# A hybrid attention and RWKV-7 trunk: the next head pair's front moved one round ahead, small products alternating between tiles of the PE array

## The chip, the cores and the metric

The kernel runs on one core of a Trainium2 chip. The metric is the device time of one execution in microseconds. Its engines are named as in the profile: PE (TensorE matmul), DVE (VectorE), ACT (ScalarE), POOL (GpSimd), SP (the DMA queue). Each runs its own list of instructions in program order; semaphores join them.

## The reference

Two layers over x (512 tokens, 1024 channels). A layer normalizes x, projects it once, and feeds two groups whose outputs are joined and projected back: softmax attention (4 heads) and a bidirectional RWKV-7 time mixing (8 heads of 64). A gated MLP with a width-3 convolution follows. The part that the change touches is the RWKV group:

```python
def wkv7_scan(r, w, k, v, kk, a, reverse):
    def step(state, inp):
        r_t, w_t, k_t, v_t, kk_t, a_t = inp
        sa = jnp.einsum('bhvk,bhk->bhv', state, -kk_t)
        state = (state * w_t[:, :, None, :] + sa[..., None] * (kk_t * a_t)[:, :, None, :]
                 + v_t[..., None] * k_t[:, :, None, :])
        return state, jnp.einsum('bhvk,bhk->bhv', state, r_t)
    ...
def direction(xw, xa, d, reverse):
    w = rwkv_decay(xw, w0[d], w2[d])            # exp(-exp(-softplus(-(w0 + tanh(xw) @ w2)) - 0.5))
    a = jax.nn.sigmoid(a0[d] + xa @ a2[d])
    k_d = k * (1 + (a - 1) * k_a)
    return wkv7_scan(heads(r), heads(w), heads(k_d), heads(v), kk, heads(a), reverse), k_d
```

The outputs of both directions are summed, normalized per head, given a bonus from r, k and v, and gated.

## The kernel before

Channels lie on partitions, tokens along the free dimension. The 512 RWKV channels are four blocks of 128, each with one pair of heads (e = 0, 1); each pair is scanned forwards and backwards (d = 0, 1). The scan is chunked: 8 chunks (NCH) of 64 tokens (C). For one block the work has these parts.

- **The front.** PE multiplies the decay and rate inputs by their low-rank weights (`rwkv_early`, L517, banks 1 and 2), ACT takes the tanh (L984, L991) and adds one (L986), DVE sums the decays along each chunk (`decay_sum`, L1412, a scan over 512 columns for each d), ACT takes both exponentials (`grown` L996, `shrunk` L1001) and the key factor (`factor`, L1006). DVE forms queries (`queries`, L1419 to L1425), removals (`removals`, L1430, L1433), keys and the bonus (L1438 to L1446).
- **The triangle.** PE forms the 32x32 blocks of each chunk's triangular matrix (`rwkv_triangle`, L531, 32 products for each d, in banks 5 and 6), which ACT copies to `LB` (L1018).
- **The inverse.** DVE inverts these blocks (`inverse_in` L1473, a 32x32 transposition, then `inverse_8`, `inverse_16_*`, `inverse_32_*`, and the transposition back in `inverse_out`, L1551). ACT helps with copies (L1027, L1033, L1035).
- **The level.** PE completes the 64x64 inverse from the 32x32 blocks (`rwkv_level`): 32 transpositions X (L551), 32 products T (L557), 32 products Z (L567). ACT copies each result out in two halves, d or e (`level`, L1047, L1052, L1059, and the diagonal blocks, L1040). Grams (L588), tokens (L600 to L603) and values (L610) of the first two chunks lie between.
- **The scan.** Eight steps s, each a chain through three engines: PE's state product (L625), ACT's copy R (L1072), PE's solve (L640), ACT's copy SA (L1079, two halves), PE's update S (L650), DVE's decayed state (`scan_state`, L1568), and the next step. Values, grams, tokens and output products (L610, L588, L600, L656) fill PE between them, and DVE masks the grams (`scan_ring`, L1562).
- **The tail.** The output is copied by ACT (L1086); PE centres it (L664), sums the squares (L669) and computes the gate (L674), each 512 columns wide; ACT squares, takes Ln (L1101) and Exp (L1106), with a table load each; DVE joins them (`tail_norm`, L1575 to L1579).

A software pipeline written out by hand in three functions named `rwkv_round`, one for each engine, sets the order. A layer has five rounds, cur = -1 to 3, named so below. Round cur scans block cur, builds block cur + 1 (triangle and inverse, spread over the scan's steps; then, after the scan, the level), and ends the tail of block cur - 1. At the end of the round, after the scan's last product, PE issues the low-rank products of block cur + 2. Its DVE part, the front proper, is issued at the start of round cur + 1. Round -1 has no scan, round 3 nothing to build.

What waits for what around the change: the level's transpositions wait for `inverse_out` (semaphore inv_v) and, before, for the tanh of the next block's rate (ear_a A1), because the low-rank products use the level's banks. The next round's first solve waits for ACT's copies of Z and of the first values.

The buffers: CW and PP (summed decays and their exponential) lay in columns that the inverse uses as scratch (LTMP), so a block's front could not run beside another block's inverse.

## Time and profile before

| | us |
|---|---|
| median of 3 runs | 1926.53 (1922.97 to 1933.13) |
| the profiled execution's own time | 1921.93 |
| its span from first to last instruction | 1920.0 |
| RWKV rounds 0 to 3 of layer 0, first solve to last output product | 334.43 to 529.44 |
| the same of layer 1 | 1268.88 to 1464.29 |
| busy: PE, DVE, ACT, POOL | 1686.8, 1011.2, 731.6, 289.0 |
| mean granted clock of TensorE (1 is full) | 0.902 |

Times in the trace are microseconds from the span's start. A view by stretch gives for each engine its busy time and in brackets the number of instructions; PEclk is the granted clock, where 1.00 stands for 2.4 GHz and 0.50 for 1.2 GHz. In the timelines a row merges neighbouring instructions of one line: start, time from the first's start to the last's end, engine, line, operation, output and inputs, shape, count, and in square brackets what the engine idled for. One product of 32-bit floats leaves two MATMUL records.

### The profile page before, as it was taken

The page shows a single profiled execution, that of the slowest core. Times are in us where ns is not written, and L with a number is a line of the kernel's source. Part 1 is how long each engine was busy: PE and PEld are TensorE (multiplying, and loading weights), DVE is VectorE, ACT ScalarE, POOL GpSimd, SP SyncE. Part 2 cuts the span into 40 slices and gives each one's busy share as a digit, 9 for nine tenths or more (in the row PEclk, how much of TensorE's full clock was granted, in tenths as well). Part 3 has the DMA queues.
Part 4 walks back from the last instruction along what each step waited for, and adds up shares of the span by engine and source line. Part 5 has one row for each costly group of instructions (what it writes and reads, how often), then busy time and mean ns, then how long its engine had stood idle before and what let it go on. Part 6 is the DMA issues. An engine that isn't in the chain of part 4 may idle for free.

```text
span 1920.0 us, 27840 instructions
## 1 busy us (share of the span) xinstructions
PE 1686.8 (88%) x11192; PEld 1254.9 (65%) x11192; DVE 1011.2 (53%) x1533; ACT 731.6 (38%) x1193; POOL 289.0 (15%) x124
## 2 busy tenths in 40 slices
PE   2997865988998999999989978588889899999997
PEld 0784434766766888877757834276666688887785
DVE  6654557767416677664443244676653354445333
ACT  3434244556533322322233343455555332233222
POOL 1341000000021222211224400000000222222221
PEclk8998985788899999999989989677689999999999
DMA  7344110000032545543303310000002122222231
GB/s 285 137 159 145 58 61 1 2 2 2 2 121 95 201 175 186 203 146 144 123 11 122 97 55 0 1 2 2 2 2 78 55 88 91 106 87 89 86 103 72
DMA packets 34652, 162.98 MB, mean 85 GB/s; under 512 B 3840, under 2 KB 4096, under 8 KB 25856
## 3 DMA queue, kind: packets, MB, share of 16 engines
q1 hardware_dynamic: 34560, 161.65, 23.8%
q8 instruction: 70, 1.15, 0.2%
q14 instruction: 22, 0.18, 0.0%
HBM read 159.54 MB, written 2.10 MB: 84 GB/s over the span
## 4 chain that ended last, share of the span: by engine, by line
PE 58%; issue 25%; DVE 7%; ACT 5%; POOL 3%; DMA 1%; POOLq 0%; DVEq 0%; ACTq 0%; SPq 0%
PE bank L497 7%; PE bank L499 7%; PE bank L498 7%; PE bank_pair L497 3%; PE bank_pair L499 3%; PE bank_pair L498 3%; PE bank_pair L588 2%; POOL work_parts L1873 2%; PE bank L815 2%; PE bank L816 2%; PE bank L793 1%; PE bank L517 1%; PE bank L557 1%; PE bank L567 1%; PE bank L600 1%
## 5 line engine op out<-in xcount | busy, mean ns | idle before, releaser
L497 PE MATMUL bank<-work_parts,y_mix_parts 128*128 128x512 f32 x792 | 315.2, 398 | 21.3 <-DVE work_parts L1645 10.3
L499 PE MATMUL bank<-work_parts 128*128 128x512 f32 x792 | 314.5, 397 | 0.0
L1658 DVE TENSOR_TENSOR work_parts<-work,y_mix_parts 128x1024 fp32r<-128x1024 f32 x66 | 169.2, 2564 | 258.1 <-ACT y_mix_parts L941 258.1
L1868 POOL TENSOR_TENSOR proj_weights_parts<-proj_weights,proj_weights_hi 128x1024 fp32r<-128x1024 f32 x54 | 130.1, 2418 | 990.4 <-ACT proj_weights_hi L937 914.9
L1873 POOL TENSOR_TENSOR work_parts<-work,y_mix_parts 128x1024 fp32r<-128x1024 f32 x66 | 158.7, 2405 | 608.4 <-ACT y_mix_parts L941 608.4
L941 ACT ACTIVATE y_mix_parts<-work 128x1024 fp32r<-128x1024 f32 x132 | 133.0, 1054 | 263.9 <-DMA work<-mlp_dram 254.2
L498 PE MATMUL bank<-work_parts,y_mix_parts 128*128 128x512 f32 x528 | 208.7, 395 | 0.0
L497 PEld LDWEIGHTS bank<-work_parts,y_mix_parts 128*128 128x128 f32 x792 | 150.5, 190 | 59.2 <-issue 25.0
L499 PEld LDWEIGHTS bank<-work_parts 128*128 128x128 f32 x792 | 150.1, 190 | 35.5
L497 PE MATMUL bank<-work_parts,proj_weights_hi 128*128 128x512 f32 x272 | 111.8, 411 | 26.3 <-DVE work_parts L1645 23.8
L498 PEld LDWEIGHTS bank<-work_parts,y_mix_parts 128*128 128x128 f32 x528 | 99.8, 189 | 24.1
L499 PE MATMUL bank<-work_parts,proj_weights_parts 128*128 128x512 f32 x272 | 109.1, 401 | 0.0
L499 PE MATMUL bank_pair<-work_parts 128*128 128x512 f32 x264 | 104.7, 397 | 0.0
L498 PE MATMUL bank<-mixer_inputs_parts,y_mix_parts 128*128 (+1 forms) x264 | 104.6, 396 | 0.0
L497 PE MATMUL bank_pair<-work_parts,y_mix_parts 128*128 128x512 f32 x264 | 104.4, 395 | 0.0
L1301 ACT ACTIVATE work<-work 128x512 f32<-128x512 f32 x44 | 27.8, 633 | 156.1 <-DVE work L1808 156.1
L1344 DVE CUSTOM_DVE_ANT_0 work<-work,c_act 128x1024 f32<-128x1024 f32 x64 | 77.6, 1249 | 12.2 <-DMA work<-ada_dram 12.1
L498 PE MATMUL bank<-work_parts,proj_weights_hi 128*128 128x512 f32 x208 | 83.5, 401 | 0.0
L497 PEld LDWEIGHTS bank<-work_parts,proj_weights_hi 128*128 128x128 f32 x272 | 52.7, 194 | 44.0 <-issue 26.4
L517 PE MATMUL bank<-mixer_inputs 64*128 64x512 f32 x64 | 41.0, 1043 | 37.2 <-ACT work L984 21.2
L497 PE MATMUL bank_pair<-work_parts,proj_weights_hi 128*128 128x512 f32 x160 | 68.5, 428 | 4.7 <-POOL proj_weights_parts L1868 4.7
L498 PE MATMUL bank_pair<-work_parts,y_mix_parts 128*128 128x512 f32 x176 | 69.1, 393 | 0.0
(262 smaller groups left out, 3116.3 us busy)
## 6 DMA issues: line engine op xcount, KB each, us to landing
work<-mlp_dram SPq DMA_DIRECT2D x66, 1024.0 KB, 4.8
work<-ada_dram SPq DMA_DIRECT2D x64, 512.0 KB, 4.7
proj_weights<-tiles_dram SPq DMA_DIRECT2D x57, 512.0 KB, 3.6
x_res<-ada_dram SPq DMA_DIRECT2D x24, 512.0 KB, 4.7
x_res<-x_dram SPq DMA_DIRECT2D x2, 2048.0 KB, 10.4
mixer_inputs<-ada_dram SPq DMA_DIRECT2D x8, 512.0 KB, 17.3
work<-mlaw_dram SPq DMA_DIRECT2D x4, 640.0 KB, 4.3
out_dram<-x_res SPq DMA_DIRECT2D x8, 256.0 KB, 2.2
```

The costliest lines, as they stand in the source:

```text
L497: mm(out, w_hi, x_hi, start=start, stop=False)
L498: mm(out, w_hi, x_lo, start=False, stop=False)
L499: return mm(out, w_lo, x_hi, start=False, stop=stop)
L517: own(ear_p, mm(PS[1 + d][:, :], l_rw[rows, b, i, :], mix(x)[rows, :], start=True, stop=True), f"{n}{d}")
L588: last = mm(PS[3 + e][:, d * P:(d + 1) * P], BK[p][d][rows, s, :, :], ZR[p][d][rows, s, :, :], start=True, stop=True)
L815: mm(bank[:, :], QN[:, e, qb * P:(qb + 1) * P], KN[:, e, :], start=True, stop=False)
L816: mm(bank[:, :], QPE[:, qb * P:(qb + 1) * P], KPE[e], start=False, stop=True).then_inc(att_p.sem, att_p.one(f"sc{i}"))
L941: F(MW_H[q][:, half], MW_IN[q][:, half], ACT.Identity).then_inc(msp_a.sem, msp_a.one(f"h{half}"))
L1344: dve.tensor_tensor_reduce(out=slots[u], in0=slots[u], in1=CACT, scale=0.5, scalar=0.0, op0=ALU.mult, op1=ALU.add, accum_out=dots[:, u:u + ...
L1658: TTT(MW_L[q][:, 1], MW_IN[q][:, 1], plain(MW_H[q][:, 1]), ALU.subtract).then_inc(msp_v.sem, msp_v.one("l1"))
L1868: pool.tensor_tensor(ring_l[s], ring[s], plain(ring_h[s]), ALU.subtract).then_inc(spl_q.sem, spl_q.one(f"t{s}"))
L1873: pool.tensor_tensor(MW_L[q][:, 0], MW_IN[q][:, 0], plain(MW_H[q][:, 0]), ALU.subtract).then_inc(msp_q.sem, msp_q.one("l0"))
```

## The change

It does six things.

1. **The low-rank products** move from between two rounds into steps 4 and 6 of the scan, from banks 1 and 2 to 5 and 6 (`rwkv_early`, now in two halves). ACT's tanh, shift and rate follow in steps 5, 6 and 7.
2. **The front** of block cur + 2 runs a round ahead: `decay_sum` in step 7 on DVE, before the end of the inverse; the exponentials and factors on ACT right after the scan (`factors`), before the level's copies; queries, removals, keys and bonus on DVE after the inverse.
3. **The triangle products** of block cur + 2 stand in the level of block cur + 1: those of d = 0 behind the T products, those of d = 1 behind the Z products. In the next round ACT copies those of d = 1 in step 0, between the copies R and SA, and the inverse starts in step 0 in place of step 2.
4. **The T and Z products**: a product of d = 0 (e = 0) and one of d = 1 (e = 1) alternate, with outputs in different partitions: T now in 32 to 63 and 96 to 127; Z as before in 0 to 31 and 64 to 95. Both halves of T wait for the copy X1, and the halves of each end together.
5. **The tail** moves forward: centre in step 0, variance in step 2, Ln in step 3, Exp in step 6; the gate goes behind the scan, before the level. The centred output gets a copy of its own on ACT ("cp", 512 columns), so that banks 5 and 6 are free. `tail_norm` runs at the end of the same round.
6. **Buffers**: CW lies where PI lies, PP in the ring of the high weight halves.

Round -1 has the same shape: the first block's front and triangle stand before it, and the second block's front in it.

```diff
-        RING_H = sb("proj_weights_hi", 3 * KD * P, F32R)
+        RING_P, RING_H = two_names("proj_weights_hi", 3 * KD * P)
+        CW, PP = PI, [RING_P[:, 512 * d:512 * d + 512] for d in range(2)]
...
@@ PE @@
             def rwkv_level(it, b, scan, early):
                 pe.wait_ge(inv_v.sem, inv_v.at("out", it))
-                if early:
-                    pe.wait_ge(ear_a.sem, ear_a.at("A1", it + 1))
-                elif scan:
+                if scan:
...
-                for d in D2:
-                    pe.wait_ge(lev_a.sem, lev_a.at(f"X{d}", it))
-                    for m in range(16 * d, 16 * d + 16):
-                        last = mm(PS[1 + d][32:64, (m % 16) * 32:(m % 16) * 32 + 32], LB[0:32, m, 32:64], X0T[0:32, m, :],
+                pe.wait_ge(lev_a.sem, lev_a.at("X1", it))
+                for i in range(16):
+                    for d in D2:
+                        m = 16 * d + i
+                        ins = mm(PS[1 + d][64 * d + 32:64 * d + 64, i * 32:i * 32 + 32], LB[0:32, m, 32:64], X0T[0:32, m, :],
...
+                if early:
+                    rwkv_triangle(it + 1, 0)
                 scan_values(it, 0)
                 scan_tokens(it, b, 1)
...
-                for e in range(2):
-                    for d in D2:
-                        for c in range(NCH):
+                for d in D2:
+                    for c in range(NCH):
+                        for e in range(2):
...
+                if early:
+                    rwkv_triangle(it + 1, 1)
...
-                    if build and s in (0, 1):
-                        rwkv_triangle(new, s)
-                    if build and s == 3:
+                    if trail and s == 0:
+                        if build:
+                            pe.wait_ge(tri_a.sem, tri_a.at("B10", new))
+                        tail_centre(old)
+                    if build and s == 0:
                         rwkv_bonus(new)
...
+                    if early and s == 4:
+                        rwkv_early(new + 1, nxt + 1, 0)
+                    if early and s == 6:
+                        rwkv_early(new + 1, nxt + 1, 1)
...
-                if early:
-                    rwkv_early(new + 1, nxt + 1, scan)
                 if build:
                     scan_gram(new, 0)
                     scan_tokens(new, nxt, 0)
+                    if trail:
+                        if early:
+                            pe.wait_ge(ear_a.sem, ear_a.at("A1", new + 1))
+                        tail_gate(old, cur - 1)
                     rwkv_level(new, nxt, scan, early)
@@ ACT @@
                         if s < NCH - 1:
                             scan_ring(it, s + 1)
+                    if build and s == 0:
+                        triangle(new, 1)
+                    if scan:
                         scan_solve(it, s)
...
                 if scan:
                     tail_take(it)
                 if early:
-                    for d in D2:
-                        early_decay(new + 1, nxt + 1, d)
-                    for d in D2:
-                        early_rate(new + 1, nxt + 1, d)
+                    factors(new + 1, nxt + 1)
                 if build:
                     scan_ring(new, 0)
-                    level(new, nxt + 1)
+                    level(new, early)
@@ DVE @@
                 for s in range(NCH):
                     if scan and s < NCH - 1:
-                        scan_ring(it, s + 1)
+                        scan_state(it, s)
+                    if scan and s < NCH - 2:
+                        scan_ring(it, s + 2)
                     if build:
                         if s == 0:
-                            keys(new, nxt, 0)
-                            keys(new, nxt, 1)
+                            inverse_in(new)
+                            inverse_half(new)
...
+                        if s == 7:
+                            if early:
+                                for d in D2:
+                                    decay_sum(new + 1, d)
+                            inverse_32_end(new)
+                            inverse_out(new)
...
+                if build:
+                    scan_ring(new, 0)
+                    if trail:
+                        tail_norm(old, cur - 1)
+                    if early:
+                        queries(new + 1, nxt + 1, 0)
+                        removals(new + 1, nxt + 1, 0)
+                    for q in range(2):
+                        diagonal(new, q)
+                    if early:
+                        queries(new + 1, nxt + 1, 1)
+                        removals(new + 1, nxt + 1, 1)
+                    scan_ring(new, 1)
+                    if early:
+                        front_sums(new + 1, nxt + 1)
```

How it moves instructions, at three places of layer 0, at the end of round 1. Each list is one engine's order; a bracket names the semaphores waited for. **PE, from the scan's last product to the level's transpositions, before:**

```order
L517 MATMUL bank<-mixer_inputs 128x512 [waits tl_a,sc_a,lora_in]
L517 MATMUL bank<-mixer_inputs 128x512
L517 MATMUL bank<-mixer_inputs 128x512 [waits ear_a] x2
L588 MATMUL bank_pair<-work 128x128 [waits pre_v,sc_v]
L588 MATMUL bank_pair<-work 128x128 x3
L600 MATMUL bank<-constants,work 128x128 [waits vr_a,sc_a]
L600 MATMUL bank<-constants,work 128x128
L602 MATMUL bank<-constants,mixer_inputs 128x128
L603 MATMUL bank<-constants,work 128x128
L551 MATMUL bank<-constants,work 32x32 [waits ear_a,inv_v]
L551 MATMUL bank<-constants,work 32x32 x31
```

and now:

```order
L590 MATMUL bank_pair<-work 128x128 [waits pre_v,sc_v]
L590 MATMUL bank_pair<-work 128x128 x3
L602 MATMUL bank<-constants,work 128x128 [waits vr_a,sc_a]
L602 MATMUL bank<-constants,work 128x128
L604 MATMUL bank<-constants,mixer_inputs 128x128
L605 MATMUL bank<-constants,work 128x128
L676 MATMUL bank<-mixer_inputs 128x512 [waits tl_a,ear_a]
L546 MATMUL bank<-constants,work 32x32 [waits tl_a,sc_a,inv_v]
L546 MATMUL bank<-constants,work 32x32 x31
```

The four low-rank products (L517) and their waits for ACT's tanh (ear_a) are gone from here; the gate (L676) has come in, with a wait for ear_a that the scan's last steps fill; the transpositions (L551, now L546) wait for the inverse. **PE, from the T products (L557, now L553) to the Z products (L567, now L566), before:**

```order
L557 MATMUL bank<-work 32x32 [waits lev_a]
L557 MATMUL bank<-work 32x32 x15
L557 MATMUL bank<-work 32x32 [waits lev_a]
L557 MATMUL bank<-work 32x32 x15
L610 MATMUL bank<-work 64x64 [waits sc_a,sc_v]
L610 MATMUL bank<-work 64x64 x3
L600 MATMUL bank<-constants,work 128x128 [waits sc_a]
L600 MATMUL bank<-constants,work 128x128
L602 MATMUL bank<-constants,mixer_inputs 128x128
L603 MATMUL bank<-constants,work 128x128
L567 MATMUL bank<-work 32x32 [waits lev_a]
L567 MATMUL bank<-work 32x32 x31
```

and now:

```order
L553 MATMUL bank<-work 32x32 [waits lev_a]
L553 MATMUL bank<-work 32x32 x31
L528 MATMUL bank<-work 32x64 [waits tl_v,ear_a,pre_v]
L528 MATMUL bank<-work 32x64 x31
L612 MATMUL bank<-work 64x64 [waits sc_a,sc_v]
L612 MATMUL bank<-work 64x64 x3
L602 MATMUL bank<-constants,work 128x128 [waits sc_a]
L602 MATMUL bank<-constants,work 128x128
L604 MATMUL bank<-constants,mixer_inputs 128x128
L605 MATMUL bank<-constants,work 128x128
L566 MATMUL bank<-work 32x32 [waits lev_a]
L566 MATMUL bank<-work 32x32 x31
```

T no longer waits halfway, and the 32 triangle products of d = 0 (L528) stand behind it, with a wait for the removals of the next block (pre_v); the other 32 follow the Z products, before the next round's first solve. **DVE, from the transposition that ends the inverse (L1551, now L1561) on, before:**

```order
L1551 STREAM_TRANSPOSE work<-lane_inverse 64x32x32 [waits inv_v,lev_p,lev_a]
L1562 TENSOR_TENSOR work<-bank_pair,constants 128x512 [waits sc_p]
L1412 SCALAR_TENSOR_TENSOR work<-constants,work 128x512 [waits ear_a] x2
L1419 TENSOR_TENSOR work<-mixer_inputs,work 128x8x63 [waits pre_a]
L1420 COPY work<-mixer_inputs 128x8
L1422 TENSOR_TENSOR work<-mixer_inputs,work 128x8x64
L1425 COPY chunk_ends<-work 128x8
L1557 COPY work<-work 32x16x32 [waits inv_v] x2
L1419 TENSOR_TENSOR work<-mixer_inputs,work 128x8x63 [waits pre_a]
L1420 COPY work<-mixer_inputs 128x8
L1424 TENSOR_TENSOR work<-mixer_inputs,work 128x8x64
```

and now, from the two rows before it:

```order
L1422 SCALAR_TENSOR_TENSOR work<-constants,work 128x512 [waits ear_a] x2
L1551 TENSOR_REDUCE lane_inverse<-work 128x8x8 [waits inv_v] x2
L1553 COPY lane_inverse<-lane_inverse 64x8x16 [waits inv_v]
L1561 STREAM_TRANSPOSE work<-lane_inverse 64x32x32 [waits inv_v,lev_p,lev_a]
L1572 TENSOR_TENSOR work<-bank_pair,constants 128x512 [waits sc_p]
L1585 SCALAR_TENSOR_TENSOR squares<-mixer_inputs,params,squares 128x512 [waits tl_a,tl_p]
L1587 SCALAR_TENSOR_TENSOR squares<-squares,params,y_mix 128x512 [waits tl_v]
L1589 TENSOR_TENSOR y_mix<-squares,bank 128x512 [waits tl_v]
L1429 TENSOR_TENSOR work<-mixer_inputs,proj_weights_hi 128x8x63 [waits pre_a,sc_p]
L1430 COPY work<-mixer_inputs 128x8
L1432 TENSOR_TENSOR work<-mixer_inputs,proj_weights_hi 128x8x64
```

The decay sums (L1412, now L1422) have moved ahead of the inverse's end; `tail_norm` (L1585 to L1589) now stands between the first gram's mask (L1572) and the next block's queries (L1429 on).

## Rows read from the trace of the kernel before

**Rows 1.** The page, part 1: busy time of each engine.
```profile
PE 1686.8 (88%) x11192; PEld 1254.9 (65%) x11192; DVE 1011.2 (53%) x1533; ACT 731.6 (38%) x1193; POOL 289.0 (15%) x124
```

**Rows 2.** Busy by stretch, layer 0: length, PE, PEld, DVE, ACT, POOL, PEclk.
```profile
334.43:364.33 29.90, 27.98 (x534) 22.76 (x534) 22.09 (x44) 14.91 (x38) 0.00 (x0) 0.90 0.01 2
364.33:375.95 11.62, 9.07 (x60) 5.02 (x54) 6.96 (x9) 5.50 (x10) 0.00 (x0) 0.64 0.01 1
375.95:389.20 13.25, 11.62 (x181) 10.66 (x180) 8.80 (x17) 8.00 (x15) 0.00 (x0) 0.50 0.01 2
389.20:422.80 33.60, 29.92 (x536) 23.51 (x538) 22.16 (x44) 19.38 (x44) 0.00 (x0) 0.91 0.01 2
422.80:436.04 13.24, 10.89 (x62) 5.72 (x59) 6.89 (x9) 5.50 (x10) 0.00 (x0) 0.63 0.01 1
436.04:446.89 10.85, 9.22 (x181) 8.40 (x180) 9.41 (x18) 7.86 (x15) 0.00 (x0) 0.65 0.01 2
446.89:481.28 34.39, 29.78 (x536) 23.30 (x538) 23.71 (x47) 19.38 (x44) 0.00 (x0) 0.90 0.01 2
481.28:487.68 6.40, 5.17 (x54) 2.85 (x51) 6.11 (x8) 1.81 (x5) 0.00 (x0) 0.81 0.01 3
487.68:498.84 11.16, 9.53 (x180) 8.71 (x180) 3.98 (x7) 5.21 (x11) 0.00 (x0) 0.63 0.01 2
```

**Rows 3.** The same view, layer 1: rounds 0 and 1 whole.
```profile
1268.88:1321.50 52.62, 46.60 (x767) 37.21 (x767) 37.82 (x68) 28.43 (x63) 0.00 (x0) 0.79 0.01 2
1321.50:1381.53 60.03, 52.36 (x772) 39.61 (x772) 38.45 (x69) 32.87 (x69) 0.00 (x0) 0.76 0.01 2
```

**Rows 4.** Timeline of PE from round 1's end: start, duration, line, operation.
```profile
428.53 1.55 PE L517 MATMUL bank<-mixer_inputs 64*128 64x512 f32 x4 [0.79 <-ACT squares L1086]
...
436.04 1.10 PE L551 MATMUL bank<-constants,work 32*32 32x32 f32 x32
...
437.72 2.51 PE L557 MATMUL bank<-work 32*32 32x32 f32 x64
...
441.83 3.43 PE L567 MATMUL bank<-work 32*32 32x32 f32 x64
```

**Rows 5.** Timeline of PE inside round 1's scan: products between tiles.
```profile
391.46 0.64 PE L650 MATMUL bank<-work 128*64 128x64 f32 x8
...
391.88 0.64 PE L656 MATMUL bank<-work 128*64 128x64 f32 x8
...
399.10 1.10 PE L531 MATMUL bank<-work 64*32 64x64 f32 x64
...
409.30 1.02 PE L664 MATMUL bank<-squares,constants 128*128 128x512 f32 x2
```

**Rows 6.** Timeline of DVE in round 1.
```profile
413.04 0.29 DVE L1568 TENSOR_TENSOR rstd<-bank,chunk_ends 128x128 f32<-128x128 f32 x1 [0.61 <-PE bank L650]
...
416.53 0.29 DVE L1568 TENSOR_TENSOR rstd<-bank,chunk_ends 128x128 f32<-128x128 f32 x1 [0.40 <-PE bank L650]
...
435.75 2.33 DVE L1412 TENSOR_TENSOR_SCAN work<-constants,work 128x512 f32<-128x512 f32 x2
...
438.33 0.68 DVE L1419 TENSOR_TENSOR work<-mixer_inputs,work 128x504 f32<-128x504 f32 x1 [0.25 <-ACT work L996]
...
441.92 0.68 DVE L1430 SCALAR_TENSOR_TENSOR work<-work,mixer_inputs 128x512 f32<-128x512 f32 x1
...
445.60 0.74 DVE L1575 SCALAR_TENSOR_TENSOR squares<-bank,params,squares 128x512 f32<-128x512 f32 x1
```

**Rows 7.** Timeline of ACT in round 1.
```profile
390.52 1.52 ACT L1006 ACTIVATE work<-work,derived 128x512 f32<-128x512 f32 x2
...
407.59 1.28 ACT L932 ACT_TABLE_LOAD   x1
...
431.45 0.67 ACT L984 ACTIVATE work<-bank,derived 128x512 f32<-128x512 f32 x1
...
436.71 1.07 ACT L1047 ACTIVATE work<-bank 32x512 f32<-32x512 f32 x2
```

243 lines of the change are left out of this document (116 added, 127 removed).

## The prediction

> **What bounds the kernel now.** The page comes first: PE is busy for 88% of the span [rows 1], so the place where it is not is what an edit of the order can win. The RWKV rounds of the two layers take two times some 195 us; all else is left as it is. I cut each round of layer 0 at three marks, to be seen in the view by stretch [rows 2]: its first solve, the seventh and last decayed state (S6), the level's first transposition, and the next round's first solve. For rounds 0, 1 and 2 the stretches are 29.90, 11.62, 13.25; 33.60, 13.24, 10.85; and 34.39, 6.40, 11.16 us. The reader is to see two things. In the scan (first stretch) the granted clock is 0.90 to 0.91 and PE is nearly always busy: the chain of a step goes from PE to ACT to PE to ACT to PE to DVE, a step with little else in it takes 416.53 - 413.04 = 3.49 us [rows 6], and what PE or ACT do beside it mostly adds to it. In the other two stretches the clock is 0.50 to 0.65 except in round 2 (0.81 and 0.63), and PE has 54 to 62 records between S6 and the transpositions: it waits there, for the low-rank products and ACT's tanh. These two run from 428.53 to 436.04 in round 1, 7.5 us [rows 4]; round 2, which has no next block, needs 6.40 where round 1 needs 13.24.
>
> **S6 to the transpositions.** The round trip between PE and ACT goes. Late next is DVE's inverse. In round 2 it is what the transpositions wait for already, so 6.40 us is the length of that chain. In rounds 0 and 1 two decay sums, 2.33 us [rows 6], now stand in it: 8.7. ACT has in the same time the rate's two tanh, the output's copy, four exponentials and two factors: eight or nine operations of some 0.67 us [rows 7] end about 6 us after the scan's last product, which the inverse covers to within a fraction; the low-rank weights were loaded long before. Gains: 11.62 - 8.7 = 2.9; 13.24 - 8.7 = 4.5; round 2: 0.
>
> **The transpositions to the next solve.** PE has X, a gram, T, in rounds 0 and 1 the triangle of d = 0, values and tokens, then Z; ACT then copies Z twice, the diagonal and R (some 2.1 us), and the triangle of d = 1 lies in that gap. T took 2.51 us partly at the full clock and Z 3.43 at half, for 64 records each, 54 ns a record of 32 columns [rows 4]. For products that alternate between tiles beside each other in the array's columns the nearest rows are the updates at half clock: 391.88 - 391.46 = 0.42 us for 8 records of 64 columns, 53 ns each [rows 5], so half as much for a column. I take T and Z at half: 1.0 us each at the full clock, 1.7 at half. The triangle costs 1.10 at full [rows 5], some 1.9 at half. Given back: T's two copies and Z's two copies, 1.07 a pair [rows 7], now stand behind the whole product, 0.5 each.
>
> The page TensorE: Matmul & The Clock Gate of the Trainium skill, section The mechanism, has a rule against this: weight loads overlap running products only where the row group differs, and here both tiles share their rows. By that rule T and Z would gain nothing. The updates share all their rows, too, and their 53 ns for 64 columns speak against it.
>
> Triangle 0 waits for DVE, which after the inverse masks a gram (0.6), in rounds 1 and 2 joins the tail (three operations of 0.74, 2.2), then forms queries (1.35) and removals (1.3), each from operations of 0.68 [rows 6]: ready at 3.3 us in round 0 and 5.4 in round 1. T ends at 2.9 (full clock) to 4.5 (half), so round 1 waits 0.9 us or more. The sum of PE's pieces and the last copies is in round 0 8.4 us at full and 11.8 at half clock, in round 1 10.6 to 12.8, in round 2, without triangles, 7.3 to 10. These are the ends. The stretch was at 0.50 to 0.65 before and is denser now; I take 10.5, 12 and 9.2. Gains: 2.7; -1.2; 2.0.
>
> **The scan, first solve to S6.** Seven steps of 3.49 are 24.4; with the first at half clock 25.3. What lies beside: ACT's copies of the second triangle between R and SA, two operations, some 0.8 beyond the idle that they fill; a product of 512 columns 1.02 at full clock [rows 5] and twice that at half, so the bonus in step 0 1.3, the centre there (rounds 1, 2) 1.3, the variance 0.9 and the first low-rank pair 0.9. ACT has about 1.9 us free in a step. In step 1 of rounds 1 and 2 it has an inverse copy, a table load of 1.28 [rows 7], a small Ln, the square and the new copy, together 3.1: 1.2 too long. In step 5 of round 1 it loads a table for two tanh, 2.7: 0.8 too long. Sums: round 0 25.3 + 0.8 + 1.3 + 0.9, and 0.4 for DVE's longest piece of the inverse, 28.7; round 1 32.5; round 2 30.8 (it has two products in step 0 at the clock of the level's end, 2.6). Gone are both triangles (1.1 each), DVE's transposition ahead of the third decayed state, and the stall of the Exp's table load behind the Ln, moved to where the step has room. Gains: 1.2, 1.1, 3.6.
>
> **Around them.** The first round (-1) has the decay sums ahead of its level, 2.3 more, and gets back 1.3 from T and Z: -1.0. Round 3 has the centre at half clock and one copy more on ACT in step 1: -0.8. Instruction loads, the DMA queue and POOL do not change: I cost them at nothing, as SP's only work here are weights that wait for the tail's end.
>
> **The sum.** Layer 0: round 0 2.9 + 2.7 + 1.2 = 6.8; round 1 4.5 - 1.2 + 1.1 = 4.4; round 2 0 + 2.0 + 3.6 = 5.6; less 1.8: 15.0. Layer 1 has 52.62 and 60.03 us for rounds 0 and 1 [rows 3]; against the new 47.9 and 53.2 that is 4.7 and 6.8, with round 2 as in layer 0 and less 1.8: 15.3. Together 30. The profiled execution took 1921.9, the median of the runs is 4.6 above it: 1892 for its like, **1896** for the median. With every stretch at its full-clock end the gain is 45 to 50, with every one at its half-clock end 20 to 25.
>
> **The rivals.**
> - *The tiles do not overlap* (the rule above), chance 0.12. Then T and Z keep 2.0 to 3.4 us, and each level loses what was counted for them and its copies behind whole products, some 2.4 us in eight levels, 19 us: 1915. For it: the two tiles read the same 32 partitions. Against it: the updates' rows.
> - *The clock pays more*, 0.13. The stretches at 0.50 [rows 2] are those where PE waited; if they run at full speed now, another 15: 1881.
> - *The work only moves*, 0.08. The scan fills with low-rank products, shifts and table loads, each on the chain; if every operation moved into it costs its whole length (ACT's 3.1 and 2.7 us, shift and Exp in step 6 2.1, PE's products at half clock) the scans lose 4 to 5 us each, and 1926 is left. For it: PE and ACT alternate without slack in a step. Against it: the 1.9 us of ACT's idle.
> - *The triangle blocks the level*, 0.05, slower. PE takes its list in order: values, tokens, Z and the next solve are queued behind triangle 0, and triangle 1 stands before the solve. Both wait for DVE's front, 14 operations of 0.68 with the tail's. It decides from the point where the removals of d = 0 come more than some 5 us after T's end, not 0.9: if DVE's whole front (keys and bonus too, 4 us) and ACT's factors stood ahead of it. Then the level of six rounds is 7 us longer than forecast, 42 in all: 1938. Against it: DVE's order has the removals of d = 0 right behind the tail.
>
> **How the numbers follow.** The forecast (1884 to 1908) has 0.62. A measurement of this kernel tells about 0.5%, 9.6 us, from no change. Faster by more (under 1917): forecast, clock, and most of the tiles' rival, 0.84. Within: 0.11. Slower: 0.05. The range 1876 to 1914 takes in the clock's rival and the lower end of the sum, and leaves out the slow half of the tiles' rival and the last two.
>
> **What would show it.** In the profile after: no low-rank products between scan and level, transpositions 8.7 us after S6 in rounds 0 and 1 (PE idle there for DVE, not ACT); T and Z at 1.0 to 1.7 us; PE idle before triangle 0 in round 1 only, by 1 to 3 us; the scan's steps 1 and 5 longest, with ACT as what PE waits for; the inverse's first transposition some 4 us after the first solve, not 12. It is wrong if T and Z keep 54 ns a record, if the scan stretches do not shorten, or if PE's idle before triangle 0 exceeds 4 us.

## The result, and the profile after

The changed kernel takes **1875.93 us** (median of 4 runs, 1868.62 to 1877.95); the kernel before, run beside it, 1924.75. The ratio is 0.9739 (95% interval 0.9689 to 0.9788): 49 us faster, where 30 were forecast. The time lies just under the low end of the range (1876). The profiled execution of the change took 1874.6 us, its span is 1872.7; the span before was 1920.0, so 47.3 us are to be found in the two traces.

The page, part 1, of the kernel after; it answers to [rows 1]:

```profile
PE 1646.2 (88%) x11192; PEld 1226.1 (65%) x11192; DVE 1007.9 (54%) x1533; ACT 730.4 (39%) x1201; POOL 289.3 (15%) x124
```

PE has the same 11192 records in 40.6 us less busy time: part of the gain is that the products themselves take less time, some by their order and some by the clock (its mean is 0.915, before 0.902). The view by stretch, layer 0, cut at the same marks as [rows 2] (first solve, S6, transpositions, next first solve), with the scan of round 3 as the last row:

```profile
333.78:359.67 25.89, 25.62 (x410) 20.19 (x410) 18.12 (x37) 14.14 (x38) 0.00 (x0) 0.93 0.01 2
359.67:368.26 8.59, 3.99 (x57) 2.47 (x51) 8.30 (x10) 7.01 (x15) 0.00 (x0) 0.98 0.01 2
368.26:380.75 12.49, 12.12 (x308) 10.82 (x308) 11.13 (x22) 6.37 (x13) 0.00 (x0) 0.50 0.01 3
380.75:409.96 29.21, 27.95 (x414) 21.27 (x414) 18.23 (x38) 18.46 (x44) 0.00 (x0) 0.93 0.01 2
409.96:418.54 8.58, 4.84 (x59) 2.73 (x53) 8.29 (x10) 7.52 (x15) 0.00 (x0) 1.00 0.01 2
418.54:431.60 13.06, 11.75 (x308) 10.38 (x308) 12.75 (x25) 6.38 (x13) 0.00 (x0) 0.52 0.01 3
431.60:459.56 27.96, 26.92 (x410) 21.04 (x410) 18.67 (x39) 16.02 (x40) 0.00 (x0) 0.92 0.01 2
459.56:466.17 6.61, 5.08 (x54) 2.97 (x48) 6.32 (x8) 3.39 (x7) 0.00 (x0) 0.80 0.01 4
466.17:474.20 8.03, 5.44 (x182) 4.73 (x181) 3.81 (x7) 5.00 (x10) 0.00 (x0) 0.93 0.01 2
474.20:502.54 28.34, 27.74 (x410) 21.07 (x410) 7.73 (x17) 17.13 (x40) 0.00 (x0) 0.89 0.01 2
```

Beside the forecast, in us:

| layer 0 | before | forecast | after |
|---|---|---|---|
| round 0: scan / S6 to transpositions / to next solve | 29.9 / 11.6 / 13.3 | 28.7 / 8.7 / 10.5 | 25.9 / 8.6 / 12.5 |
| round 1 | 33.6 / 13.2 / 10.9 | 32.5 / 8.7 / 12 | 29.2 / 8.6 / 13.1 |
| round 2 | 34.4 / 6.4 / 11.2 | 30.8 / 6.4 / 9.2 | 28.0 / 6.6 / 8.0 |
| around (round -1, round 3): gain | | -1.0, -0.8 | +0.65, -0.5 |

The middle stretch came as forecast to 0.2 us. In it DVE is busy all the time and PE idles until the inverse's last transposition (the first row below). The level of rounds 0 and 1 is longer than forecast, at a mean granted clock of 0.50 and 0.52. The scans are 3 us shorter than forecast each, and that is nearly the whole surprise; the gains around the rounds and the losses in the levels cancel. Layer 1 repeats it: rounds 0 and 1 take 47.12 and 50.93 us, where [rows 3] have 52.62 and 60.03.

Timeline of PE in the level of round 1:

```profile
418.54 1.44 PE L546 MATMUL bank<-constants,work 32*32 32x32 f32 x32 [2.94 <-DVE work L1561]
...
421.06 1.92 PE L553 MATMUL bank<-work 32*32 32x32 f32 x64
423.92 1.93 PE L528 MATMUL bank<-work 64*32 64x64 f32 x64 [0.94 <-DVE work L1443]
...
427.45 1.92 PE L566 MATMUL bank<-work 32*32 32x32 f32 x64
429.30 1.93 PE L528 MATMUL bank<-work 64*32 64x64 f32 x64
431.60 0.69 PE L642 MATMUL bank<-rstd,work 64*64 64x64 f32 x8 [0.38 <-ACT rstd L1091]
```

T (L553) and Z (L566) take 1.92 us for 64 records at half clock, where [rows 4] have 3.43 for Z. PE waits 0.94 us for the removals ahead of the first triangle, as forecast; the second triangle ends 0.4 us before the solve may start, so the gap between Z and the solve is filled.

### The profile page after: what moved, and what is told of

It reads as the page before. It is cut to its first block, busy times and chain, and to the rows that moved or that the text cites. A ratio compares the mean times of both kernels' runs of the same rounds, so it can differ in the third digit from the quotient of the medians.

```text
span 1872.7 us, 27854 instructions
## 1 busy us (share of the span) xinstructions
PE 1646.2 (88%) x11192; PEld 1226.1 (65%) x11192; DVE 1007.9 (54%) x1533; ACT 730.4 (39%) x1201; POOL 289.3 (15%) x124
## 4 chain that ended last, share of the span: by engine, by line
PE 57%; issue 25%; DVE 8%; ACT 5%; POOL 3%; DMA 2%; POOLq 0%; DVEq 0%; SPq 0%; ACTq 0%
PE bank L498 7%; PE bank L500 7%; PE bank L499 7%; PE bank_pair L498 4%; PE bank_pair L500 3%; PE bank_pair L499 3%; POOL work_parts L1901 2%; PE bank_pair L590 2%; PE bank L821 2%; PE bank L822 2%; PE bank L642 1%; PE bank L799 1%; PE bank L602 1%; PE bank L612 1%; DMA proj_weights<-tiles_dram 1%
## 5 line engine op out<-in xcount | busy, mean ns | idle before, releaser
L1896 POOL TENSOR_TENSOR proj_weights_parts<-proj_weights,proj_weights_hi_parts 128x1024 fp32r<-128x1024 f32 x54 | 130.1, 2415 | 942.4 <-ACT proj_weights_hi_parts L947 866.3
L498 PE MATMUL bank<-work_parts,proj_weights_hi_parts 128*128 128x512 f32 x272 | 112.0, 412 | 26.3 <-DVE work_parts L1667 23.7
L1354 DVE CUSTOM_DVE_ANT_0 work<-work,c_act 128x1024 f32<-128x1024 f32 x64 | 77.6, 1250 | 12.2 <-DMA work<-ada_dram 12.1
L499 PE MATMUL bank<-work_parts,proj_weights_hi_parts 128*128 128x512 f32 x208 | 83.5, 401 | 0.0
L498 PEld LDWEIGHTS bank<-work_parts,proj_weights_hi_parts 128*128 128x128 f32 x272 | 52.7, 194 | 44.0 <-issue 26.3
L1578 DVE TENSOR_TENSOR rstd<-bank,chunk_ends 128x128 f32<-128x128 f32 x56 | 16.3, 291 | 106.7 <-PE bank L652 106.7
L498 PE MATMUL bank_pair<-work_parts,proj_weights_hi_parts 128*128 128x512 f32 x160 | 68.6, 429 | 4.4 <-POOL proj_weights_parts L1896 4.4
## 6 DMA issues: line engine op xcount, KB each, us to landing
x_res<-x_dram SPq DMA_DIRECT2D x2, 2048.0 KB, 10.5
```

Of the source, the lines that this page charges most:

```text
L498: mm(out, w_hi, x_hi, start=start, stop=False)
L499: mm(out, w_hi, x_lo, start=False, stop=False)
L1354: dve.tensor_tensor_reduce(out=slots[u], in0=slots[u], in1=CACT, scale=0.5, scalar=0.0, op0=ALU.mult, op1=ALU.add, accum_out=dots[:, u:u + ...
L1896: pool.tensor_tensor(ring_l[s], ring[s], plain(ring_h[s]), ALU.subtract).then_inc(spl_q.sem, spl_q.one(f"t{s}"))
```

## The experiments

Beside the medians I use one sum from the traces: from a layer's first solve to its last output product, both layers together. It is 390.3 us before and 343.3 after. A difference between two changed kernels is smaller than either's difference from the kernel before: the 95% intervals of the products in turn, of the late low-rank products, of the filled idle time and of the earlier inverse all overlap the change's (0.9689 to 0.9788). There the reading rests on the traces.

**Products in turn.** In the change, T and Z back to one tile after the other:

```diff
-                for i in range(16):
-                    for d in D2:
+                for d in D2:
+                    for i in range(16):
...
+                for e in range(2):
                 for d in D2:
                     for c in range(NCH):
-                        for e in range(2):
```

> The changed kernel, but the T products of d = 0 all before those of d = 1, and the Z products of e = 0 before those of e = 1 (outputs in the same partitions as in the change). Theory A (products that alternate between tiles beside each other run at twice the rate, and that is part of the gain): T and Z go back from 1.92 us to about 3.4 us for 64 records at half clock and from 1.20 to about 2.0 at full clock; the copies overlap again, about 0.5 us each. Each of the six levels at half clock gets 2.0 us longer, the two at full clock 0.7, less 0.9 in round 1, where the triangle waited for DVE anyway: some 12 us, 1888 us. Theory B (alternation changes nothing, the gain is all from the order): 1876 us within 3, and T and Z at 1.92 us still.

Measured: 1884.89 us, ratio 0.9792 (0.9744 to 0.9841). Timeline of PE, round 0's level of this run:

```profile
375.39 3.43 PE L553 MATMUL bank<-work 32*32 32x32 f32 x64
```

**Alternation alone.** The kernel before with the alternation only (T into partitions 64d + 32 to 64d + 63, both copies of T behind all of it).

> The kernel before with only the alternation of T and Z between the tiles (and the copies that go with it). Theory A: T and Z take 1.9 us at half clock in place of 2.5 to 3.4; a level wins 3.0 and gives back 1.0 for copies that stand behind whole products: 2.0 us in each of eight levels (0.7 where the clock is up), 13 us, about 1911 us. Theory B (DVE's front and ACT's exponentials, which stand in the level of the kernel before, take over the level): T and Z as short, but PE idles for them, 1920 to 1925 us.

Measured: 1910.75 us, ratio 0.9928 (0.9906 to 0.9951). The same place there:

```profile
376.25 1.92 PE L558 MATMUL bank<-work 32*32 32x32 f32 x64
```

Theory A holds from both sides: 3.43 against 1.92 us for the same 64 records, 9 us worse between the medians without it in the change, 14 us better with it in the kernel before. With the levels of round -1 added, the traces put it at 13.1 and 12.2 us. What these two runs do not separate: the products that alternate between tiles also alternate between two PSUM banks (`PS[1]` and `PS[2]`), and no run alternates only one of the two. The updates of the scan, which alternate between tiles within one bank, took 53 ns for 64 columns [rows 5] where T and Z in turn took 54 ns for 32; this speaks for the tiles, but is no test.

**DVE's state first.** The kernel before; the decayed state moved up within each step:

```diff
                     if scan and s < NCH - 1:
                         scan_ring(it, s + 1)
+                        scan_state(it, s)
                     if build:
...
-                    if scan and s < NCH - 1:
-                        scan_state(it, s)
```

> The kernel before with one thing changed on DVE: in each step of the scan the decayed state comes right behind the gram's mask, ahead of keys, bonus and the pieces of the inverse. Theory A (PE's own queue covers the late first state: it is busy with the first triangle until the state product): the first stretch to the first decayed state falls from 4.83 us to 2.94, the stretch behind it grows by as much, and only the step with DVE's transposition wins about 1 us: 6 us in six rounds, 1919 us. Theory B (the held state is on the path in both steps): 2.9 us in each of six rounds, 1908 us.

Measured: **1953.57 us**, ratio 1.0155 (1.0108 to 1.0201), slower by 29: neither theory. The first stretch is 2.94 us and the step behind it longer by as much, as theory A has it; but the four steps after it take 4.9 to 6.8 us. PE's waits in round 1's scan of this run:

```profile
PE bank L640 <- ACT rstd L1072: 4.1, 4, 1.9
PE bank_pair L588 <- DVE work L1562: 3.4, 2, 2.0
```

The second row is new. Each piece of the inverse now stands, on DVE, between the state of one step and the mask (L1562) of the next; PE's next gram (L588) waits for that mask, and values and the update stand behind the gram. Before, the piece stood behind the mask and cost only what it held of the state. The scans of rounds 0 to 2 together are 13.6 us longer in layer 0 for it; most of the rest of the loss is in levels that now run wholly at 0.50 (13.25 us in each round) and in round 2's transpositions, 8.65 us after S6.

**DVE's order of the change, alone.** The kernel before, with the mask one step further ahead as well:

```diff
+                if scan:
+                    scan_ring(it, 1)
                 for s in range(NCH):
                     if scan and s < NCH - 1:
-                        scan_ring(it, s + 1)
+                        scan_state(it, s)
+                    if scan and s < NCH - 2:
+                        scan_ring(it, s + 2)
...
-                    if scan and s < NCH - 1:
-                        scan_state(it, s)
```

> The kernel before with DVE's order of the change in the scan: the decayed state first in each step and the gram's mask one step further ahead (that of step 1 is made before the scan). Theory A (e3_state_first lost 29 us because each piece then stood ahead of the mask for which PE's values, and behind them the update, wait; with the mask a step ahead that wait is gone): none of the 5 to 6 us steps of that run; the step with DVE's transposition falls from 6.33 us to 4.5 to 5.5, the others stay, some 9 us less than before in six rounds, about 1915 us. Theory B (the pieces hold the next state as much as they held this one): 1921 to 1930 us.

Measured: 1924.98 us, ratio 1.0 (0.9985 to 1.0016): theory B's time, though the steps move as theory A has it. With the mask a step ahead, three of the steps that took 5.58, 6.74 and 5.00 us in round 1 of the state-first run take 4.01, 4.69 and 3.49, which bears out the reading above. The scans do get 0.9 to 2.1 us shorter in layer 0, but the inverse, begun in step 2, ends later: in round 2 PE idles 3.88 us before the transpositions, which come 8.66 us after S6 in place of 6.40, and the level behind them takes 13.25 us at half clock in place of 11.16.

```profile
492.35 1.88 PE L551 MATMUL bank<-constants,work 32*32 32x32 f32 x32 [3.88 <-DVE work L1551]
```

So DVE's order brings nothing by itself here: what the scans win, the later end of the inverse and the levels take back. In the change the inverse begins in step 0, for which the front must be a round ahead; that this is what makes the order pay is argued and not tested by itself. The parts of the change are not a sum of gains.

**The second triangle in the scan.** The change, with the triangle of d = 1 moved from the gap behind Z to step 0, and ACT's copies of it behind SA.

> The changed kernel, but the 32 triangle products of d = 1 stand in step 0 of the next scan (behind the tokens, before the centre), and ACT's two copies of them behind SA in place of between R and SA. Theory A (the gap between Z and the solve is free for them, and the copies between R and SA cost nothing): the next solve comes at the same time, the first stretch stays 2.94 us, and the scans of rounds 0 to 2 get 1.1 to 1.9 us longer each, 7 to 11 us, about 1885 us. Theory B (they delay the solve or the copies delay SA by what they now save): the level gets shorter by 0.8 us or more, and the time stays within 3 us of 1876.

Measured: 1891.54 us, ratio 0.9824 (0.9797 to 0.9851), 16 us more than the change (13.8 in the sum of the traces), and more than PE's own time makes (7 to 11). Rounds 0 and 1: level 12.5 us both, first stretch 2.94 still, but the step behind it 7.28 and 8.29 us in place of 4.60 and 5.85. Timelines of PE and DVE from round 1's step 0 on:

```profile
385.66 1.52 PE L528 MATMUL bank<-work 64*32 64x64 f32 x64
387.89 1.12 PE L664 MATMUL bank<-squares,constants 128*128 128x512 f32 x2 [0.72 <-ACT work L1033]
...
384.51 0.68 DVE L1574 TENSOR_TENSOR rstd<-bank_pair,constants 128x512 f32<-128x512 f32 x1
388.48 1.92 DVE L1485 STREAM_TRANSPOSE work<-work 64x1024 f32<-64x1024 f32 x1 [3.29 <-ACT work L1033]
...
392.59 0.29 DVE L1580 TENSOR_TENSOR rstd<-bank,chunk_ends 128x128 f32<-128x128 f32 x1 [1.87 <-PE bank L650]
```

DVE's transposition waits 3.3 us for ACT's copies of the triangle (L1033), but it does not hold the next decayed state: DVE idles 1.87 us before that, for PE's update (L650). What is long is PE's own queue. The triangle takes 1.52 us in it, and behind it the centre (L664) waits another 0.72 us for the same copies; in round 0, where there is no centre, the bonus waits 1.28 us. The state product stands behind them. To PE's time, which I had priced, comes this wait for the copies, which I had not.

**The low-rank products behind the scan again.** The change, with both pairs, the tanh and the shift behind the last output product.

> The changed kernel with the low-rank products, the tanh and the shift again behind the scan's last product, everything else a round ahead as in the change. Theory A (the round trip between PE and ACT is on the path there, and DVE's decay sums and with them the inverse's end now stand behind it): from S6 to the transpositions about 15 us in rounds 0 and 1 in place of 8.6, the triangle of d = 0 later still, and the scan 1.5 us shorter: 5 to 9 us a round in four rounds, 1896 to 1912 us. Theory B (what the low-rank work costs in the scan is as much as it costs behind it): within 5 us of 1876.

Measured: 1886.85 us, ratio 0.9789 (0.9759 to 0.9819): 11 us more than the change between the medians, 15.9 in the sum of the traces. From S6 to the transpositions 12.41 and 12.98 us, the scan 1.0 shorter. DVE's waits there, round 1:

```profile
DVE work L1418 <- ACT work L999: 4.3, 1, 4.3
```

The decay sums (L1418) wait 4.3 us for the shift, with the inverse's end behind them. Theory A's mechanism, with a smaller size: the time lies below its range and 6 us above theory B's.

**PE's idle time filled.** The change, with products of 128x512, whose results are overwritten, between gate and transpositions.

```diff
+                    if early and scan:
+                        pe.wait_ge(sc_a.sem, sc_a.at(f"SA{NCH - 1}", it))
+                        for _ in range(3 if trail else 4):
+                            mm(PS[1][:, :], ident, mix(XG), start=True, stop=True)
                     rwkv_level(new, nxt, scan, early)
```

> The changed kernel with three more 128x512 products (four in round 0) on PE between the gate and the transpositions of rounds 0 and 1, where PE idles 3 to 4.6 us for DVE's inverse; their results are overwritten. Theory A (the idle time brings the granted clock down to 0.50 for the level, and work in it keeps the clock up): transpositions still 8.6 us after S6, and from there to the next solve 9 to 10 us in place of 12.5 and 13.1, at a clock above 0.9: 13 us less, about 1863 us. Theory B (the level's small products bring the clock down by themselves): the level stays at 0.50, and the time at 1876 to 1880 us.

Measured: 1864.52 us, ratio 0.9704 (0.9661 to 0.9747); the sum of the traces is 337.0, 6.3 less than the change. The medians differ by 11.4, but the rest is not shown to come from the filling: 1.2 us of it are in the levels of round -1, which are not filled here (0.64 and 0.63 in place of 0.50), and some 4 lie outside the rounds. By stretch, levels of rounds 0 and 1:

```profile
367.39:377.46 10.07, 8.59 (x309) 7.54 (x309) 9.87 (x21) 6.25 (x13) 0.00 (x0) 0.83 0.02 4
414.10:427.18 13.08, 10.27 (x309) 8.99 (x309) 12.78 (x25) 6.24 (x13) 0.00 (x0) 0.66 0.01 3
```

In round 0 theory A holds in the main: same transpositions, 8.6 us after S6, but a level of 10.07 us at 0.83 in place of 12.49 at 0.50 (forecast above 0.9). In round 1 the clock is full until T ends; then PE idles for the first triangle, longer than before because T ended sooner, and that triangle runs at half clock. That the wait brings the clock down is not shown: in round 0 the same triangle runs at half clock behind a wait of 0.22 us. First row round 0, then round 1:

```profile
370.61 1.93 PE L528 MATMUL bank<-work 64*32 64x64 f32 x64 [0.22 <-DVE work L1447]
...
415.89 1.20 PE L553 MATMUL bank<-work 32*32 32x32 f32 x64
419.49 1.93 PE L528 MATMUL bank<-work 64*32 64x64 f32 x64 [2.39 <-DVE work L1447]
```

Round 1's level is as long as the change's (13.08 and 13.06 us) at 0.66 and at 0.52: there DVE, busy for 12.8 us of it with a front that carries the tail's 2.2 us as well, sets it at either clock.

**A way on: the inverse earlier.** From the change, with the pieces of the inverse packed up to a step earlier, and ACT's factors behind the copies X0 and X1:

```diff
@@ DVE, steps 1 to 7 @@
-                            inverse_8(new, 1, 5)
+                            inverse_8(new, 1, 8)
                         if s == 2:
-                            inverse_8(new, 5, 8)
                             inverse_16_first(new)
-                        if s == 3:
                             inverse_16_second(new)
                             inverse_16_end(new)
-                        if s == 4:
+                        if s == 3:
                             inverse_32_first(new)
...
+                        if s == 6:
+                            inverse_32_end(new)
                         if s == 7:
...
-                            inverse_32_end(new)
                             inverse_out(new)
@@ ACT, level @@
+                if early:
+                    for d in D2:
+                        factor(it + 1, b, d)
```

> The changed kernel with the pieces of DVE's inverse packed earlier in the scan (the last two products in step 5, the last sums in step 6 ahead of the decay sums), and on ACT the copies of the transposed blocks ahead of the two key factors. Theory A (DVE's chain behind S6 sets the transpositions): S6 to the transpositions 6.6 us in place of 8.6 in rounds 0 and 1 and 5.0 in place of 6.6 in round 2; with PE idle for less than 1 us the clock may stay up in the level, another 3 us in each of rounds 0 and 1: 1853 to 1865 us. Theory B (the pieces do not fit into DVE's idle time in the steps and hold the next decayed states, or ACT's exponentials set the level): the scan gets longer by what is won, 1873 to 1880 us.

Measured: 1859.86 us, ratio 0.9665 (0.9639 to 0.9691). The transpositions come 6.65 and 6.69 us after S6, as expected; in round 2 they come 6.86 and 5.33 us after it in the two layers, where 5.0 was expected. The levels take 11.1 and 12.5 us, which is 1.4 and 0.5 less and not 3. The scan of round 0 is 1.4 us longer, those of rounds 1 and 2 0.5 to 1.4 shorter. The sum of the traces is 328.1. Theory A, with a smaller gain in the levels.

**Another order in the level.** From that kernel: both triangles behind Z, the bonus sums in the next step 0.

> v1_inverse_earlier with another order in the level: on PE values and tokens right behind T, then Z, then both triangles; on ACT the copies of the first triangle behind those of Z; on DVE the two bonus sums in step 0 of the next scan, behind the first decayed state. Theory A (in rounds -1 to 1 the first triangle, which waits up to 2.2 us for DVE, holds values, tokens and Z): Z right behind ACT's copies of T, the stretch from the transpositions to the next solve 1 us shorter in rounds -1 and 0 and 2.5 in round 1, about 9 us, 1851 us. Theory B (DVE's front sets the next solve in any order, since both triangles now stand between Z and the solve): the stretch stays at 11 to 12.5 us, 1858 to 1862 us.

Measured: 1870.6 us, ratio 0.9711 (0.9683 to 0.9739), 11 us worse than the kernel it comes from; both theories missed it. Only round 1's level is shorter (10.82 in place of 12.53). The triangles use the same two banks, and with no work between them the second waits for ACT's copies of the first, which now stand behind those of Z; and the bonus product waits for DVE, so that the step to the second decayed state takes 6.17 us in rounds 0 to 2 (4.8 to 5.7 in layer 0 of the kernel that it comes from). PE's waits in round -1's level:

```profile
PE bank L528 <- ACT work L1032: 1.3, 1, 1.3
```

**The same, filled.**

> v2_level_order with products of 128x512 on PE ahead of the transpositions, their results overwritten: four in round -1, two in round 0, one in round 1. Theory A (what brings the clock down is PE's idle time, as e5_filled showed for round 0): the level of round -1, at 0.50 until now, runs above 0.8 and takes 9 to 10 us in place of 12.5 or 11.5, round 0 by 1 us less: 6 us below v2_level_order. Theory B: four products are too few after 6 us of idle time at half clock; they only delay the transpositions: 0 to 4 us above v2_level_order.

Measured: 1860.14 us, ratio 0.9655 (0.9627 to 0.9683), 10 us below the kernel without the products. Theory A, but in round -1 only in part: its level takes 11.79 us at 0.61. There the clock fell while T ran, and Z ran at half clock; why, these runs leave open. Nor is it shown that the products raised the clock in round -1: its level ran at 0.64 and 0.63 in the filled run above, which has none there.

**The inverse earlier, filled; then values first.** Four, two and one products ahead of the transpositions of rounds -1, 0 and 1 of the kernel with the earlier inverse; and on top of it

```diff
-                if early:
-                    rwkv_triangle(it + 1, 0)
                 scan_values(it, 0)
                 scan_tokens(it, b, 1)
+                if early:
+                    rwkv_triangle(it + 1, 0)
```

> v1_inverse_earlier with products of 128x512 on PE ahead of the transpositions (four in round -1, two in round 0, one in round 1), their results overwritten. Theory A (the filled idle time keeps the clock up in the level and in the next scan's first step, as in v3_filled against v2_level_order, where it was worth 10 us): the level of rounds -1 and 0 0.7 to 1.5 us shorter, 1849 to 1855 us. Theory B (in v1_inverse_earlier the clock is up where it matters already): 1858 to 1862 us.

> v4_earlier_filled with values and tokens on PE ahead of the first triangle (which stays ahead of Z) in the level. Theory A (in round 1 PE idles 2.2 us before the triangle, for DVE's removals, with values and tokens queued behind it): the stretch from the transpositions to the next solve 1.0 to 1.5 us shorter in round 1 and the same in rounds -1 and 0, 2 to 3 us less than v4_earlier_filled in all. Theory B (they then wait for ACT's copy of the tokens and the mask of the first gram, and the triangle comes later in rounds -1 and 0): equal to v4_earlier_filled, or 1 to 3 us longer.

Measured: 1856.91 us, ratio 0.9658 (0.9638 to 0.9678), and **1851.17 us**, ratio 0.963 (0.9605 to 0.9655). The first cannot be told from the kernel without the products (0.9665), and the sums of the traces are the same (328.4 and 328.1): theory B in the total, 1 us below its range, but not for its reason. Its level of round 0:

```profile
368.89:377.70 8.81, 7.43 (x309) 6.38 (x309) 8.64 (x19) 8.15 (x16) 0.00 (x0) 1.00 0.02 5
```

That is 2.3 us less than without the products (11.12 at 0.69), more than theory A asked for. What is won there is lost behind it in layer 0 (round 1's scan 29.6 in place of 28.0 us, its level 13.1 in place of 12.5), and round -1 stays at 0.50 in that layer in spite of its four products. The second is the best measured, 25 us below the change, with an interval clear of the change's. Against the first the intervals overlap, and its profiled execution was the longer one (1857.6 against 1855.7); the sum of the traces is 3.9 us less, of which the levels of round 1 are 2.5, as theory A has it. Its levels of rounds 0 and 1:

```profile
367.58:376.36 8.78, 7.36 (x309) 6.39 (x309) 8.61 (x19) 8.17 (x16) 0.00 (x0) 1.00 0.02 5
...
411.03:422.43 11.40, 9.55 (x308) 8.49 (x308) 11.16 (x22) 8.16 (x16) 0.00 (x0) 0.72 0.01 4
```

Round 0's level runs at full clock from end to end as in the first, 8.8 us where the change has 12.5; in round 1 values and tokens fill part of the wait for DVE (13.08 and 12.19 us in the two layers before, 11.40 now). The sum of the traces is 324.5 us, against 343.3 of the change.

## Why the prediction was wrong

**The scan: the term that failed.** "Seven steps of 3.49 are 24.4; with the first at half clock 25.3." My stretch runs from the first solve to S6. It has six whole steps, but its first piece is not one: it starts at a solve and has no state product and no copy of it. The kernel before shows what such a piece takes, in round 3, where nothing stands ahead of the state on DVE; the view by stretch, rounds 1 and 3 of the kernel before:

```profile
389.20:394.03 4.83, 4.83 (x64) 4.04 (x68) 2.59 (x5) 2.50 (x5) 0.00 (x0) 0.50 0.01 3
...
498.84:501.78 2.94, 2.94 (x38) 2.60 (x40) 0.00 (x0) 2.13 (x5) 0.00 (x0) 0.50 0.02 6
```

The 4.83 us of rounds 0 to 2 are DVE's key products, in front of the state:

```profile
391.37 0.69 DVE L1438 TENSOR_TENSOR work<-work,mixer_inputs 128x512 f32<-128x512 f32 x1 [2.78 <-ACT work L1006]
...
393.42 0.69 DVE L1440 TENSOR_TENSOR work<-work 128x512 f32<-128x512 f32 x1
394.03 0.28 DVE L1568 TENSOR_TENSOR rstd<-bank,chunk_ends 128x128 f32<-128x128 f32 x1
```

The change takes them out of step 0, and all eight scans now begin with 2.94 us. A quiet step is 3.34 us (the last step of rounds 0 and 2 after), not 3.49. So the base is 2.94 + 6 x 3.34 = 23.0, not 25.3: 2.3 us too much in each of six rounds, 14 us. Of the 2.3, 1.5 are the first piece (4.4 in the sum, 2.94 measured) and 0.9 the quiet step. The second error is in "what lies beside": 0.8 us a round for ACT's copies of the second triangle between R and SA, which cost nothing (2.94 us with them there, 2.94 with them behind SA in the run with the triangle in the scan). Together 3.1 of the 2.8 to 3.3 us that each scan missed. The rest of the term was right: round 1's step with bonus and centre is 2.5 us above a quiet one (2.6 forecast), the step with ACT's table load and copies 1.0 above (1.2), the variance 1.0 (0.9), the low-rank step 1.2 (0.9 and 0.8). What was too high is the forecast's length; it does not mean that the keys were the gain. In step 0 of the kernel before the state product was covered by PE's own queue (in the state-first run the first piece is 1.9 us shorter and the next 1.8 longer in round 1), and in the change bonus and centre have taken the triangle's place there: the first two pieces of round 1 go from 9.20 to 8.79 us, those of round 0, which has no centre, from 9.27 to 7.54.

**S6 to the transpositions: right.** 8.7, 8.7 and 6.4 forecast, 8.6, 8.6 and 6.6 measured; and late next is DVE's inverse, as said: moving it forward brought the transpositions 2 us forward.

**The level: mechanism right, size too small in rounds 0 and 1.** 10.5 and 12 forecast, 12.5 and 13.1 measured, outside the half-clock ends of 11.8 and 12.8. The stretch is "denser now" (PE is busy for 12.12 of 12.49 us in round 0, before for 11.62 of 13.25), but the clock between the levels that I took from this was wrong: PE idles 3.8 us before it in round 0 and 2.9 in round 1, and the granted clock in it is 0.50 and 0.52. T and Z took 1.92 at half clock, not 1.7. Only round 2, where PE does not wait right ahead of it, has 0.93, and wins 3.1 us in place of 2.0. The sizes for the triangle (1.93 us at half), for round 1's wait (0.94) and for the last copies (1.20 + 0.63 + 0.28) were right.

**Around.** Round -1 did not lose 1.0 but won 0.65: the decay sums are ahead of the inverse's end, but the inverse's first transposition also starts 2.2 us sooner (298.66 in place of 300.87), so the transpositions stay where they were. Round 3: 0.8 forecast, 0.5 measured.

Scan +8.9, levels -1.9, around +1.9 us a layer: 9 above the 15 forecast, twice. That the last two cancel is luck.

**The signs named.** The inverse's first transposition starts 3.8 us after round 1's first solve, before 12.3, and PE idles ahead of the first triangle in round 1, as said. The longest step is not one of the two in which ACT was to be late but the one behind step 0, with bonus and centre, 5.85 us in round 1.

**The rivals.** *Tiles that do not overlap*: fell. The rule of the Trainium skill cited in the forecast (page TensorE: Matmul & The Clock Gate, section The mechanism) would have left the two orders equal; they took 3.43 and 1.92 us, so it is not borne out here. (The change of bank that goes with the change of tile is the reservation made above.) Another page of the Trainium skill, TensorEngine Tiling (Array Packing), section Key Properties, says that different tiles load weights and multiply in parallel, with no condition on rows; by that the trace agrees. *The clock pays more* names nearly the measured time, but not its cause: in four of six forecast levels the clock did not rise. Of its 15 us the filled idle time, which leaves the order alone, won 6.3 in the rounds; the 25 us of the best kernel come from the earlier inverse, the filling and the order together, and no run gives the clock's share. *The work only moves* fell (the scans of rounds 0 to 2 are 2.7 to 6.6 us shorter); *the triangle blocks the level* showed as the 0.94 us that were forecast, though it grew to 2.2 to 2.4 us in the runs in which the rest of round 1's level got faster.

## What to carry to other kernels

Before a step's price is multiplied, look at what the first piece of the stretch holds, and read it where nothing stands in front of it: here the last round showed the bare length of a stretch that all others had with a foreign wait. When an instruction is moved forward on an in-order engine, ask what it is moved ahead of; the state alone cost 29 us, because the pieces behind it then stood ahead of a mask that another engine wanted sooner. And look at what stands behind a wait as well as at the wait: in round 0 of the change PE idled 3.8 us and then took 12.5 us at half clock for what took 10.1 once that idle time was filled.

## What the runs showed of the hardware

- 32x32 products of 32-bit floats that share their 32 rows and alternate between two column tiles, and between two PSUM banks with them: 1.92 us for 64 records at half clock and 1.20 at full, against 3.43 in one tile after the other at half.
- At the same place, with the same products, a level took 12.49 us at 0.50 behind 3.8 us of idle PE and 10.07 us at 0.83 where the idle time was filled with products nobody reads; with an earlier inverse as well, 8.81 at 1.00. It was not so everywhere: in round -1 the level ran at 0.50 in 20 of the 22 profiled levels without products ahead of it and at 0.64 and 0.63 in the other two, and at 0.50 to 0.61 in the six with them.
- ACT's Exp behind a tanh needed no table load of its own. Timeline of ACT after, round 1:

```profile
405.57 1.28 ACT L994 ACT_TABLE_LOAD   x1
406.87 1.26 ACT L994 ACTIVATE work<-bank,derived 128x512 f32<-128x512 f32 x2
...
409.31 0.62 ACT L1126 ACTIVATE squares<-squares 128x512 f32<-128x512 f32 x1
```

The load is paid with the tanh in step 5, and the tail's Exp of step 6 (L1126) has none. No load is saved by it: there are 37 in either kernel, and before it was the tanh behind the scan that had none. But before, the load stood ahead of the Exp in a step of 6.27 us, the last one before S6, which takes 3.69 now. The page ScalarE: Activation LUTs of the Trainium skill, section Table sets: the hidden batching unit, puts both functions in one set; by that the trace agrees.
